# Transformer-layer kernel on one core: reordered loads into the down product, and pair sums moved behind the table fills on VectorE

## The reference

```python
def _swiglu(x, w_gate, w_up, w_down):
    return (jax.nn.silu(x @ w_gate) * (x @ w_up)) @ w_down

h = h + FFN_RES * _swiglu(_rmsnorm(h, ffn1_norm[l]), ffn1_w_gate[l], ffn1_w_up[l], ffn1_w_down[l])
...                                  # the mixer: attention, state-space model, gates
h = h + FFN_RES * _swiglu(_rmsnorm(h, ffn2_norm[l]), ffn2_w_gate[l], ffn2_w_up[l], ffn2_w_down[l])
return _rmsnorm(h, final_norm)
```

## Time and profile before

| | |
|---|---|
| median of 3 runs | 2413.47 us |
| the profiled execution's own time | 2413.12 us |
| its span | 2411.3 us (1.8 us lie around it) |
| TensorE (PE) busy | 2178.5 us, 90% |
| VectorE (DVE) | 1484.4 us, 62% |
| ScalarE (ACT) | 913.5 us, 38% |
| GpSimd (POOL) | 586.1 us, 24% |
| granted TensorE clock, mean | 0.956 of full |

### The profile page before, as it was taken

One profiled execution on the slowest core, in us unless ns is written; L12 is line 12 of the kernel. 1 busy time (PEld: TensorE's weight loads), 2 busy tenths in 40 slices (PEclk: granted clock), 3 DMA queues, 4 the chain that ended last, 5 costly groups with the idle time before them and its releaser, 6 DMA issues. The chain is left out here.

```text
span 2411.3 us, 27675 instructions
## 1 busy us (share of the span) xinstructions
PE 2178.5 (90%) x10074; PEld 1800.0 (75%) x10074; DVE 1484.4 (62%) x2330; ACT 913.5 (38%) x1552; POOL 586.1 (24%) x494
## 2 busy tenths in 40 slices
PE   5999999999996979998958898699699999998997
PEld 4777777777885978886837776577578888886886
DVE  7786565656776228952347777451665665655777
ACT  5423323224444242153137776321433323223444
POOL 5347667720000012120002221000443333320000
PEclk8999999999997989998979999799799999999999
DMA  4423343376333364322420000151322433348333
GB/s 124 109 88 121 111 141 97 99 267 218 97 96 101 116 98 149 89 78 83 127 65 4 6 6 1 51 215 48 114 83 83 128 101 99 114 148 306 97 98 108
DMA packets 234263, 258.28 MB, mean 107 GB/s; under 512 B 34640, under 2 KB 169296, under 8 KB 233616
## 3 DMA queue, kind: packets, MB, share of 16 engines
q1 hardware_dynamic: 234128, 256.51, 33.9%
HBM read 179.89 MB, written 76.58 MB: 106 GB/s over the span
## 5 line engine op out<-in xcount | busy, mean ns | idle before, releaser
L48 PE MATMUL psum<-f_B_hi,f_A_hi 128*128 128x512 f32 x1232 | 489.0, 397 | 32.2 <-DVE f_B_lo L1049 18.4
L50 PE MATMUL psum<-f_B_hi,f_A_lo 128*128 128x512 f32 x1232 | 483.3, 392 | 0.0
L49 PE MATMUL psum<-f_B_lo,f_A_hi 128*128 128x512 f32 x1232 | 483.2, 392 | 0.0
L48 PEld LDWEIGHTS psum<-f_B_hi,f_A_hi 128*128 128x128 f32 x1232 | 233.6, 190 | 83.7 <-issue 28.4
L50 PEld LDWEIGHTS psum<-f_B_hi,f_A_lo 128*128 128x128 f32 x1232 | 233.4, 189 | 49.8
L49 PEld LDWEIGHTS psum<-f_B_lo,f_A_hi 128*128 128x128 f32 x1232 | 234.0, 190 | 47.4
L48 PE MATMUL psum<-f_wd,f_hh 128*128 128x512 f32 x616 | 243.4, 395 | 18.0 <-DVE f_wd L1066 18.0
L1282 POOL TENSOR_TENSOR f_S<-f_raw 128x512 f32<-128x512 f32 x88 | 134.5, 1528 | 474.5 <-DVE f_A_lo L1021 290.9
L920 ACT CAST f_A_hi<-f_S 128x512 fp32r<-128x512 f32 x176 | 109.5, 625 | 363.7 <-PE psum L50 355.8
L49 PE MATMUL psum<-f_wd,f_hh 128*128 128x512 f32 x616 | 242.6, 394 | 0.0
L50 PE MATMUL psum<-f_wd,f_hh 128*128 128x512 f32 x616 | 242.5, 394 | 0.0
(11 more groups left out here) (316 smaller groups left out, 4317.1 us busy)
## 6 DMA issues: line engine op xcount, KB each, us to landing
f_h_raw<-hidden SPq DMA_DIRECT2D x154, 256.0 KB, 2.6
hidden<-rows SPq DMA_DIRECT2D x44, 768.0 KB, 4.3
f_raw<-ffn_w_gate SPq DMA_DIRECT2D x44, 512.0 KB, 5.2
f_raw<-ffn_w_up SPq DMA_DIRECT2D x44, 512.0 KB, 5.1
f_wd_raw<-ffn_w_down SPq DMA_DIRECT2D x44, 512.0 KB, 11.9
rows<-x SPq DMA_DIRECT2D x16, 512.0 KB, 7.7
ga_raw<-w_in SPq DMA_DIRECT2D x16, 512.0 KB, 4.5
gates<-ga_sig SPq DMA_DIRECT2D x32, 256.0 KB, 2.2
```

What stands on the lines that cost most here:

```text
L48: pe.matmul(out, lhs_hi, rhs_hi, start=first, stop=False, skip_group_check=go_on)
L49: pe.matmul(out, lhs_hi, rhs_lo, start=False, stop=False, skip_group_check=go_on)
L50: return pe.matmul(out, lhs_lo, rhs_hi, start=False, stop=last, skip_group_check=go_on)
```

## The change

It has four parts. The names a, b, c and d are used below.

- **a, loads into the down product.** Before: 8 unit loads, 4 loads of `w_down`, the last table chunk, 18 more loads of `w_down`, the store of the last pair, units 8 to 11, the residual (and the final gain), then units from 12 on. After: the loads of `w_down` and of the units alternate in the order in which units take them, the store of the last pair stands behind load 11 of `w_down`, the last table chunk and `sync_end` stand ahead of unit 12, and the residual and the gain stand ahead of unit 22.
- **b, pair sums.** Sum 0 in slot q = 0 of the next gate matrix, sums 1 and 2 in q = 1, sum 3 in q = 2, each behind that slot's table work. After the last pair all four still come directly after the multiplication.
- **c, additions into `rows`** are shifted to later q, since the residual comes later; the final norm's first half comes two units earlier and its fourth row is scaled before the last evictions' place in the loop.
- **d, `sync_small`.** The store of a small table goes out at n = 5 instead of n = 6.

```diff
+    def sync_small(self, sp):
+        sp.wait_ge(self.s["pp"], 1)
+        sp.dma_start(self.lam8_dram, ...).then_inc(self.s["small_out"], 16)
...
-                    if n == MATS - 1:
-                        (waits; units 0 to 7; w_down 0 to 3)
-                    if tb and n >= 6:
+                    if tb and n == 5:
+                        tb.sync_small(sp)
+                    if tb and 6 <= n < MATS - 1:
                         tb.sync_chunk(sp, n - 6)
-            for k in range(4, FT):
+            (waits)
+            for k in range(FT):
                 if k % 4 == 0:
                     sp.wait_ge(s_mm, PRODUCTS * (MATS - 1) + k // 4 + 1)
+                if k % 2 == 0 and k < 16:
+                    load_unit(k // 2)
                 sp.dma_start(wd_raw[k][:], w_down[k * P:(k + 1) * P, :]).then_inc(s_wd[k // 4], 16)
-            store_pair(PAIRS - 1)
-            for v in range(8, 12): ...
+                if k == PAIRS:
+                    store_pair(PAIRS - 1)
+                if k >= PAIRS and k % 3 == 0:
+                    v = 8 + (k - 12) // 3
+                    (the waits of before)
+                    load_unit(v)
-            (residual, final gain)
             if tb:
+                tb.sync_chunk(sp, tb.CHUNKS - 1)
                 tb.sync_end(sp)
             for v in range(12, UNITS):
+                if v == 2 * PAIRS:
+                    (residual, final gain)
                 sp.wait_ge(s_dlo, 2 * (v - 7))
                 load_unit(v)
...
-                    if p and not j and q < 2:
-                        pair_sum(p - 1, q + 2)
                     tables_on(n, q)
+                    if p and not j and q < 3:
+                        for i in ((0,), (1, 2), (3,))[q]:
+                            pair_sum(p - 1, i)
...
-                    for i in range(2 if p + 1 < PAIRS else 4):
-                        pair_sum(p, i)
+                    if p + 1 == PAIRS:
+                        for i in range(4):
+                            pair_sum(p, i)
...
-                if q == 2 and 4 <= k < 8:
+                if q == 3 and 4 <= k < 8:
                     add_u1(k - 4)
-                if q == 3 and 4 <= k < 8:
+                if q == 4 and 4 <= k < 8:
                     add_u7_left(k - 4)
-                if finish and q == PRODUCTS - 1 and k >= 8:
-                    final_row(k - 8)
-            if finish:
-                final_row(3)
+                if finish and q == PRODUCTS - 1 and k >= 7:
+                    final_row(k - 7)
```

More of the change, by code:

```diff
@@ L865, in _ @@
-            if finish:
-                sp.dma_start(fgain[:], finish[0].rearrange("(a d) -> a d", a=1).broadcast_to([P, D])).then_inc(s_fgain, 16)
+                if k == PAIRS:
+                    store_pair(PAIRS - 1)
+                if k >= PAIRS and k % 3 == 0:
+                    v = 8 + (k - 12) // 3
+                    sp.wait_ge(s_dlo, 2 * (v - 7))
+                    if v == PAIRS - 1:
+                        sp.wait_ge(s_hout, 32 * PAIRS)
+                        sp.wait_ge(s_gout, 16 * PAIRS)
+                    load_unit(v)
@@ L867, in _ @@
             if tb:
+                tb.sync_chunk(sp, tb.CHUNKS - 1)
                 tb.sync_end(sp)
             for v in range(12, UNITS):
+                if v == 2 * PAIRS:
+                    for m in range(ST):
+                        sp.dma_start(rows[:, m, :], residual[m * P:(m + 1) * P, :]).then_inc(s_res, 16)
+                    if finish:
+                        sp.dma_start(fgain[:], finish[0].rearrange("(a d) -> a d", a=1).broadcast_to([P, D])).then_inc(s_fgain, 16)
                 sp.wait_ge(s_dlo, 2 * (v - 7))
@@ L1006, in _ @@
                     keep(q - 1, k)
-                if finish and q == PRODUCTS - 1 and 3 <= k < 7:
-                    final_square(k - 3)
-                if finish and q == PRODUCTS - 1 and k == 7:
+                if finish and q == PRODUCTS - 1 and k < 4:
+                    final_square(k)
+                if finish and q == PRODUCTS - 1 and k == 5:
                     last.root(act, 0, FGROUPS[0])
@@ L1182, in add_w @@
                 dve.wait_ge(s_w, i + 1)
-                into(high_right(i), u5[:, i, :], s_o22, 0, i)
+                into(high_right(i), u5[:, i, :], s_o22, 1, i)
             def add_u7(i):
                 dve.wait_ge(s_u7, i + 1)
-                into(high_right(i), u7[:, i, :], s_o22, 1, i)
+                into(high_right(i), u7[:, i, :], s_o22, 0, i)
             def add_w_low(i):
@@ L1221, in _ @@
                     combine(q, k)
-                if q == 2 and 4 <= k < 8:
+                if q == 3 and 4 <= k < 8:
                     add_u1(k - 4)
-                if q == 3 and 4 <= k < 8:
+                if q == 4 and 4 <= k < 8:
                     add_u7_left(k - 4)
-                if q == 4 and 4 <= k < 8:
-                    spread(k - 4)
                 if q == 4 and 7 <= k:
                     add_v(k - 7)
+                if q == 5 and k < 4:
+                    add_u7(k)
                 if q == 5 and 4 <= k < 8:
+                    spread(k - 4)
                     add_w(k - 4)
-                if q == 5 and 7 <= k:
-                    add_u7(k - 7)
-                if q == 6 and 3 <= k < 7:
-                    add_w_low(k - 3)
-                if finish and q == PRODUCTS - 1 and k == 6:
+                if q == 6 and 4 <= k < 8:
+                    add_w_low(k - 4)
+                if finish and q == PRODUCTS - 1 and k == 4:
                     final_var(0)
-                if finish and q == PRODUCTS - 1 and k == 7:
+                if finish and q == PRODUCTS - 1 and k == 5:
                     last.inverse(dve, 0, FGROUPS[0])
                     dve.wait_ge(s_fgain, 16)
-                if finish and q == PRODUCTS - 1 and k >= 8:
-                    final_row(k - 8)
-            if finish:
-                final_row(3)
+                if finish and q == PRODUCTS - 1 and k >= 7:
+                    final_row(k - 7)
             for i in range(QUAD):
```

7 lines of the change are left out of this document (4 added, 3 removed).

## The result

The changed kernel takes 2370.52 us (median of four, 2369.02 to 2373.03), the kernel before took 2412.38 us beside it (four, 2411.24 to 2413.73): ratio 0.9827, 95% interval 0.981 to 0.9844. The forecast was 2376 us within 2370 to 2390. The profiled execution took 2371.78 us, its span is 2370.0 us: 41.3 us less than the span of before, where the sum said 37.3.

The account below looks back on a forecast made before the run. TensorE, mostly busy, was taken to lose time to fill waits (14.2 us), unit waits (18.0 us) and low clock after stalls. Terms 16.05 + 13.5 + 6.6 + 1.2 = 37.3 us off 2413.1 gave 2376 us, range 2370 to 2390.

Parts of the forecast that it names:

- b, 16.05 us forecast: Pair ends: the low part takes over a sum's stretch beside GpSimd, the fill ends earlier; 13.4 + 1.7 + 0.95 us won.
- the low clock at 402.57: f1's gate and up: 3.69 us at 0.54 of full clock after a fill wait, to go with it; 1.7 us.
- the 0.95 us at 101.00: TensorE's wait for an addition behind three sums, now behind one, 1.2 us earlier; 0.95 us go.
- the 0.8 us left for Bz: Of TensorE's 14.2 us of fill waits, some 0.3 us stay at each of the three longest; 13.4 us go.
- a in f2 and c, 13.5 + 1.2 forecast: f2's down product: stalls at units 8 and 12 go with their clock, 13.5 us; final evictions start earlier, 1.2 us.
- a in f1, 6.6 forecast: f1's down product: stalls of 2.17 and 3.19 us go with 1.71 us of clock, less 0.5 us allowed.
- The 0.5 us allowed for unit 12: f1's down product: unit 12's load now waits behind the last chunk's stores; 0.5 us deducted from 7.07.
- the first stall stays with its clock: Each down product's third unit: stall from the last multiplication and four sums stays (3.6 us together), no gain counted.
- (1): Rival at the fill: low part or sum blocked longer by GpSimd, half of 14.2 us stays; 2383 us; chance 0.16.
- (2): Rival in the down products: at a 10% lower rate units 11 or 12 are late; 2384 us; chance 0.16.
- (3): Rival in the down products: total bytes bind whatever the order, part a's 20 us stay; 2396 us; chance 0.05.
- (4): Rival at 20 pair ends: g's later store holds VectorE if landing exceeds 7.5 us; 2438 us; chance 0.03.

Follow-up runs that it names:

- a_only: The changed kernel with VectorE's pair sums and the end of f2 as in the kernel before: 2393.23 us, ratio 0.9909 to the kernel before.
- resid_only: The kernel before with only the residual and the final gain loaded later, and the additions moved with them: 2397.61 us, ratio 0.9935.
- two_sums_ahead: The changed kernel with two pair sums instead of one ahead of the fill: 2378.57 us, ratio 0.9845 to the kernel before.
- tail_undone: The changed kernel with the end of f2 (squares, mean, scaled rows) as before: 2371.57 us, ratio 0.9826 to the kernel before.
- bd_only: The kernel before with only the moved pair sums and the earlier small table store: 2396.92 us, ratio 0.9916.
- best_loads: The changed kernel with another order of loads into the down product, sums unmoved: 2371.86 us, ratio 0.9826 to the kernel before.
- late_sums: The changed kernel with pair sums spread to slots 0, 2 and 3 and an added VectorE wait for those sums: 2413.01 us, ratio 0.9987 to the kernel before.
- last_sums_later: The changed kernel with sums 2 and 3 of the last pair moved behind slot v = 1 of the down product: 2372.53 us, ratio 0.982 to the kernel before.
- after_again: The changed kernel without edit, measured again beside the other runs: 2373.19 us, ratio 0.9826 to the kernel before.

## Why the prediction was right, and where it was off

**b, 16.05 us forecast, 15.96 measured** at the third unit of f1. Right in its steps: the low part took over the stretch, three steps of 0.6 us left the way to the fill, the low clock at 402.57 and the 0.95 us at 101.00 went, and at the pair end after that nothing was won. That the total fits to 0.1 us is luck. The stage of b itself won 16.4, and the work ahead of it, from the first matmul of f1's first product on, which the change does not touch, takes 69.6 to 72.9 us in the twelve profiles. The stage of b takes 424.5 to 425.1 us in the three with the old order of sums and 407.6 to 408.7 in the seven with the changed kernel's order. Luck, too, are the 0.8 us left for Bz: the prediction has three waits of 2.2 us of which 0.3 each stay, but the eight waits before were one of 0.62, five of 1.84 to 1.87 and two of 2.14 and 2.15, and of those seven profiles four have no wait for Bz at all. The low clock is there once in each of the three old profiles, behind one fill or another (402.57 in before, 445.96 in a_only, 447.67 in resid_only), and in none of the seven, so the 1.7 us for it were rightly counted. two_sums_ahead confirms the slope: one step of 0.6 us more costs 0.6 us at each of eight. f2's gate and up: 0 forecast, 0.1 measured.

**a in f2 and c, 13.5 + 1.2 forecast, 13.8 + 1.2 measured.** The stalls at units 8 and 12 are gone with their clock, and resid_only and a_only divide them between the two causes the prediction named. The 0.3 us over are the 0.16 us that each stall costs beyond its bracket. The count of the queue in KB was good to 0.7 us at the tightest unit: unit 11 landed 45.5 us after SyncE's first issue, where the count said 44.8, and 0.5 us were to spare in place of 1.2. c's 1.2 us show in tail_undone.

**a in f1, 6.6 forecast, 8.7 measured.** This is the term that was mis-sized, by 2.1 us. The stalls and clock counted (7.07) went. The 0.5 us allowed for unit 12, behind the last chunk's stores, came as 0.48, of which 0.2 had been lost before as well (unit 13 starts 2.90 us behind unit 12 in both, where 2.72 is the rule). 1.6 of the 2.1 us are the step "the first stall stays with its clock", which the sum has without saying so: before, the clock over the 4 us behind that stall was 0.57 and 1.6 us were lost. The stall stayed, 1.79 us as before, and the clock did not fall behind it. The prediction named this case for the lower end of its range and did not take it for its sum. Another 0.3 us are the 0.16 us of each of the two stalls, and 0.2 those of unit 13. Ten profiles hold f1's first stall of 1.79 or 1.80 us. A low clock follows it in bd_only, a_only, resid_only and two_sums_ahead, as it did in before; none in the two of the changed kernel, in best_loads, tail_undone and late_sums. In f2 it follows in resid_only and two_sums_ahead alone. The length of the stall does not decide it; what does was not settled.

**The rest, 1.5 us,** fell in the mixer, which the change does not touch. The same stretch moves by 3.2 us between the two profiles of the changed kernel, and by 5 us over all twelve, so no step answers for it, and the sum is known no better than that.

**The rivals.** (1), the fill late still, did not come; two_sums_ahead shows how near it was, one sum. (2), a load late still, did not come; the margin was 0.5 us in this trace, and last_sums_later shows the stalls that come once it is gone. (3), loads that gain nothing, falls by a_only, 0.91% faster. (4) is a true mechanism with the threshold given, 2 to 4 us away. On its price the prediction had a landing of 10.6 us behind a full queue; late_sums reached the point by a later issue instead, at 2.0 us a pair.

## What to carry to other kernels

Count from the trace what stands ahead of a waited-for instruction in its engine's row, in steps of known length: here eight waits of up to 2.2 us went with three steps of 0.6, and one more sum brought 0.6 us of each back. A queue of transfers can be counted in the same way, in KB against the need of each unit; what nobody needs yet goes behind. And where a stall is removed ask what it covered: the stall behind the last pair's sums gave the loads the time that they needed, so moving the sums alone gained nothing, moving the loads alone gained nothing, and both together took 3.6 us of waits away.

## What the runs showed of the hardware

The same stall of 1.8 us of TensorE is followed in some profiles by some 4 us whose granted clock is about 0.6 (0.62 in the row above), a stretch at 1.2 GHz and a rest at 2.4, and in others by none. A fall of the clock cannot be booked to a stall by its length. The Trainium skill ("TensorE: Matmul & The Clock Gate", Part 1: The HAM clock gate) says that the monitor runs free of the program, so that the number of slow matmuls varies from run to run. The traces agree that the same stall has two outcomes. Whether anything in the program sways them was not settled: the changed kernel, best_loads, tail_undone and late_sums kept the clock in five profiles of five, on two chips at least, but two_sums_ahead, one sum away from the changed kernel and on the chip of after_again, lost it behind both first stalls.

With the one core at work, SyncE's queue took 411 GB/s over four microseconds of f2's down product, and 384 (375 KB per us) by the prediction's count over 41 us of before. After:

```profile
2154.00:2158.00 4.00, 4.00 (x19) 3.34 (x18) 2.07 (x4) 1.55 (x3) 0.00 (x0) 1.00 1.05 411
```
